# Output product of a hybrid encoder layer: two token passes of 384 and 192 tokens in place of 320 and 256

## The reference, cut to what matters

```python
h = rmsnorm(x, p['norm_pre'])
proj = h @ p['w_in']
...
merged = (ga * (ya.astype(dt) @ p['w_proj_a']) + gb * (yb.astype(dt) @ p['w_proj_b'])
          + gc * (yc.astype(dt) @ p['w_proj_c']))
y = merged.astype(dt) @ p['w_out']
return x + rmsnorm(y, p['norm_post']), (c, n, m, s_h, s_r, shift)
```

## Time and profile before

| | |
|---|---|
| median of three runs | 2294.66 us (2294.58, 2294.66, 6939.04) |
| the profiled execution | 2294.08 us |
| its span, first to last instruction | 2292.3 us |
| mean granted clock of TensorE | 0.999 |
| TensorE matmuls busy | 2251.2 us, 98% |
| VectorE, ScalarE busy | 1271.9 us, 764.1 us |

### The profile page before, as it was taken

How to read it: one execution, slowest core, us unless ns; L and a number is a source line. 1 busy time by engine, 2 the same in 40 slices (tenths; PEclk the granted TensorE clock), 3 DMA queues, 4 the chain that set the end, 5 groups by cost and what they waited for, 6 DMA issues and landing times.

```text
span 2292.3 us, 45143 instructions
## 1 busy us (share of the span) xinstructions
PE 2251.2 (98%) x19061; PEld 2187.7 (95%) x19061; DVE 1271.9 (55%) x1978; ACT 764.1 (33%) x1159; POOL 56.5 (2%) x83
## 2 busy tenths in 40 slices
PE   5999999999999999999999999999999999999998
PEld 5999999999999999998998999989999999999998
DVE  5434443487777776663643735536557664455354
ACT  5321221234333433332422313324323343334443
POOL 0000000000000000000000000000000000000000
PEclk9999999999999999999999999999999999999999
DMA  5422222233342433411311112114221254444365
GB/s 174 140 70 94 88 76 87 73 103 119 112 142 95 137 119 124 156 60 50 106 43 65 72 49 93 61 49 149 75 86 58 90 181 147 156 144 166 141 214 189
DMA packets 65915, 249.40 MB, mean 109 GB/s; under 512 B 8922, under 2 KB 16268, under 8 KB 47892
## 3 DMA queue, kind: packets, MB, share of 16 engines
q1 hardware_dynamic: 65764, 247.14, 31.2%
HBM read 216.92 MB, written 30.19 MB: 108 GB/s over the span
## 4 chain that ended last, share of the span: by engine, by line
PE 95%; DVE 2%; DMA 1%; ACT 1%; issue 1%; SPq 0%; DVEq 0%; POOL 0%; ACTq 0%; POOLq 0%
PE acc L976 56%; PE acc L1135 12%; PE branch L1135 6%; PE acc L1526 6%; PE branch L1526 2%; PE branch L1248 1%; PE branch L1239 1%; PE branch L1223 1%; PE branch L1436 1%; DMA scratch<-in_x_all 1%; PE branch L1080 1%; DVE act_lo L2811 0%; PE branch L1073 0%; PE branch L1212 0%; PE branch L1541 0%
## 5 line engine op out<-in xcount | busy, mean ns | idle before, releaser
L976 PE MATMUL acc<-act_hi,w_hi 128*128 128x320 f32 (+3 forms) x3200 | 975.5, 305 | 1.9 <-DVE act_lo L2811 1.8
L976 PE MATMUL acc<-act_lo,w_hi 128*128 128x320 f32 (+3 forms) x3200 | 948.6, 296 | 0.0
L976 PE MATMUL acc<-act_hi,w_lo 128*128 128x320 f32 (+3 forms) x3200 | 948.1, 296 | 0.0
L976 PEld LDWEIGHTS acc<-act_hi,w_hi 128*128 128x128 f32 x3200 | 602.7, 188 | 16.8 <-issue 5.0
L976 PEld LDWEIGHTS acc<-act_lo,w_hi 128*128 128x128 f32 x3200 | 602.9, 188 | 0.7
L976 PEld LDWEIGHTS acc<-act_hi,w_lo 128*128 128x128 f32 x3200 | 602.7, 188 | 0.0
L2041 DVE TENSOR_TENSOR w_lo<-w_raw,w_hi 128x2048 fp32r<-128x2048 f32 x131 | 300.0, 2290 | 281.1 <-ACT w_hi L1573 278.6
L1573 ACT ACTIVATE w_hi<-w_raw 128x2048 fp32r<-128x2048 f32 x131 | 250.9, 1915 | 134.3 <-PE branch L1526 120.8
L1135 PE MATMUL acc<-corner_terms,w_hi 128*128 128x288 f32 x624 | 125.5, 295 | 0.0
L1135 PE MATMUL acc<-act_hi,w_hi 128*128 128x288 f32 x392 | 115.9, 296 | 1.3 <-DVE w_lo L2231 1.3
L1135 PE MATMUL acc<-act_lo,w_hi 128*128 128x288 f32 x392 | 115.7, 295 | 0.0
(11 more groups left out here) (446 smaller groups left out, 3256.5 us busy)
## 6 DMA issues: line engine op xcount, KB each, us to landing
w_raw<-in_w_stream SPq DMA_DIRECT2D x132, 1024.0 KB, 5.0
w_raw<-in_w_stream SPq DMA_DIRECT2D x76, 512.0 KB, 5.7
gate_logits<-gate_out SPq DMA_DIRECT2D x48, 288.0 KB, 2.3
scratch<-gate_logits SPq DMA_DIRECT2D x48, 288.0 KB, 5.3
scratch<-in_x_all SPq DMA_DIRECT2D x9, 512.0 KB, 6.3
branch_rows<-branch_out SPq DMA_DIRECT2D x16, 288.0 KB, 2.2
scratch<-in_x_all SPq DMA_DIRECT2D x3, 1024.0 KB, 10.5
out_y_prompt<-scratch SPq DMA_DIRECT2D x6, 512.0 KB, 2.9
```

What stands on the lines that cost most here:

```text
L976: last = mm(acc[s][:, at:at + hi - lo], a[:, s, w], b[:, k, lo:hi], start=(k == order[0] and a is whi and b is xh), stop=(k == order[-1] a ...
```

## The change

The first pass takes 384 tokens and the second 192. The 384 tokens are three full groups of 128; the 192 are one of 128 and one of 64. Everything that followed from the old cut follows the new one.

```diff
-OUT_COLS = [(0, 320), (320, KEPT)]
-OUT_ROWS = [[(0, 128), (128, 256), (256, 320)], [(320, 448), (448, KEPT)]]
+OUT_COLS = [(0, 384), (384, KEPT)]
+OUT_ROWS = [[(0, 128), (128, 256), (256, 384)], [(384, 512), (512, KEPT)]]
...
-        zt = [gbuf[0][:, 0:320], gbuf[1][:, 0:320]]
+        zt = [gbuf[0][:, 0:384], gbuf[1][:, 0:384]]
...
-                if p == 0:
-                    last = v.tensor_tensor(YT[0:64, 2, bass.ds(col, P)], br[j][0:64, 2 * P:3 * P], part[0:64], ALU.mult)
+                if p:
+                    last = v.tensor_tensor(YT[0:64, 4, bass.ds(col, P)], br[j][0:64, P:2 * P], part[0:64], ALU.mult)
...
-            v.tensor_reduce(out=small[:, 24:26], in_=squares[:, 0:2, :], axis=AX.X, op=ALU.add).then_inc(out_sums[0], 1)
-            v.tensor_reduce(out=small[0:64, 26:27], in_=squares[0:64, 2:3, :], axis=AX.X, op=ALU.add).then_inc(out_sums[0], 1)
+            v.tensor_reduce(out=small[:, 24:27], in_=squares[:, 0:3, :], axis=AX.X, op=ALU.add).then_inc(out_sums[0], 1)
...
-            v.tensor_reduce(out=small[:, 27:29], in_=squares[:, 3:5, :], axis=AX.X, op=ALU.add).then_inc(out_sums[1], 1)
+            v.tensor_reduce(out=small[:, 27:28], in_=squares[:, 3:4, :], axis=AX.X, op=ALU.add).then_inc(out_sums[1], 1)
+            v.tensor_reduce(out=small[0:64, 28:29], in_=squares[0:64, 4:5, :], axis=AX.X, op=ALU.add).then_inc(out_sums[1], 1)
...
-            pool.wait_ge(out_sums[0], 2)
+            pool.wait_ge(out_sums[0], 1)
             row_scales(0, (0, 3))
-            pool.wait_ge(out_sums[1], 1)
+            pool.wait_ge(out_sums[1], 2)
             row_scales(1, (3, 5))
```

## The result

The changed kernel takes 2315.2 us (median of 4 runs, 2312.6 to 2317.9), the kernel before 2295.3 beside it (median of 4 runs, one of which took 6939.0 us and the others 2294.6 to 2296.0): ratio 1.0084, 95% interval 1.0072 to 1.0096. So it is slower by 19.9 us, inside the 2% that were called "no change" beforehand, but clear of zero. Forecast were 2309.0 us and a range of 2301 to 2316. The profiled execution of the change took 2317.93 us, the longest of the four.

A forecast was written before the change was run, and what follows sets the result against it. TensorE's matmul stream was taken to bound the kernel. Pass one +20.3, pass two -6.2, supply +1.0 and end -0.3 sum to +14.8 us on the profiled 2294.08 us: 2309.0 us, range 2301 to 2316.

The forecast's parts named there:

- The bound: Whole run: TensorE has a matmul in flight for 2251.2 of 2292.3 us, so its stream sets the run time.
- The load floor: Pass two at 192 columns: one 128 x 128 weight load, about 110 ns, sets the matmul spacing, not the stream's 90.0.
- Pass one, +20.3 us: Output product at 384 columns: 723 matmuls on the chain each cost 28.1 ns more, +20.3 us.
- Pass two, -6.2 us: Output product at 192 columns: 768 matmuls go from 118.1 to 110 ns, -6.2 us; products of 5.50 us hide conversion.
- The supply, +1.0 us: Pass two's weight loads: TensorE waits where a landing takes over 7.4 us; +1.0 us, bounds 0 and +4.
- The end, -0.3 us: After the last product: shorter last copy, transposes and squares, last stores of 256 KB; -0.3 us, between 0 and -0.8.
- The case given 0.75: Whole run: load floor of 106 to 113 ns with little or no supply wait, 2305 to 2313 us; chance 0.75.
- the one given 0.10: Whole run: load floor near 118 ns, or a supply wait of over 3 us, 2313 to 2317 us; chance 0.10.
- Conversion decides: Pass two: no load floor, weight-tile conversion holds products at 4.8 us; 2297.8 us, or some 2302 with short supply; chance 0.09.
- no change: Both passes: matmuls cost columns plus a constant, so the paces' sum stays as now; 2292.5 us; chance 0.04.
- Load as dear as the present pace: Pass two: load floor near 118 ns, so no gain there; 2314.1 us; shares the 0.10 with long supply waits.
- The clock rival: Pass two: TensorE drops to 1.2 GHz, 171 ns a matmul, +40.6 us, about 2355 us in all; chance 0.02.

The follow-up runs named there:

- first experiment: Changed kernel with pass one's matmuls cut back to 320 columns, tokens 320 to 383 left out, pass two kept at 192: 2294.2 us, ratio 0.9994.
- the weights-only run: Changed kernel without pass two's residual loads (groups 3 to 5) and stores (groups 1 to 3), TensorE's pass-two loop written out: 2312.6 us.
- the run without stores: Changed kernel without pass two's stores of the three finished row groups, residual loads kept: 2311.7 us, ratio 1.0066.
- the wait at its use: Changed kernel with TensorE's pass-two loop written out and the wait for emptied transpose banks moved to before the transposes: 2313.7 us, ratio 1.0074.

## Why the prediction was right, point by point

**The bound.** Right: TensorE's stream is the chain, and what it gained the run gained.

**The load floor.** Right, and it is what sets the sign. The trace of before showed it at two restarts (0.11 us); the runs at 224, 192 and 128 columns show one pace, 111 to 112 ns (at 240 line and floor can't be told apart). I took 110; a product of 5.56 us against 5.50 forecast makes 16 x 0.06 = 1.0 us. The 106.7 ns of the Trainium skill ("TensorE: Matmul & The Clock Gate", section "LDWEIGHTS (loading the stationary operand)") lie some 5 ns under the measured pace. The formula of the Trainium skill, same title, section "Back-to-back issue gap", by which the sum wouldn't change, doesn't hold here: 224 columns have the pace of 128. The prediction took it alone; the same section gives it for an isolated matmul and says that in a stream of weight loads and matmuls both set the spacing, and with that the runs agree.

**Pass one, +20.3 us.** Right in mechanism, a little small: 8.777 us a product against 8.70 forecast, so +21.5 us. The line through 256, 288 and 320 columns gave 174.3 ns at 384, and 176 was measured. Why the last 64 columns cost 29.8 ns and the ones before 28.1 stays open. It isn't the third transpose, now of 128 rows: with it and 320 columns a product takes 7.35 us (first experiment). And it begins at once: 336 and 352 columns measure 154.4 and 161.0 ns, where the line has 153.2 and 160.3.

**Pass two, -6.2 us.** Half wrong. With nothing in its way it is -5.3 us (89.07 against 94.33, the weights-only run). But the step "the product of 5.50 us hides what must fit in it" failed at the loop's end: the wait `rows_taken` ends with VectorE's `rows_out`, 0.4 us behind the conversion that I did count, and the branch behind it needs more than what is left. That costs 1.7 us in the traces (90.81 - 89.07, the run without stores against the weights-only run).

**The supply, +1.0 us.** The term that was off most. In the profiled execution it is 4.2 us (95.00 - 90.81): one load after 9.6 us, where over 7.4 was named as the point from which TensorE waits. The wait behind it is longer by the branch as well. Two more things were missed: that it is the stores that delay a load, and that this wait of 2.5 us is followed by a stretch at 1.2 GHz, which costs some 1.7 us more (3.4 us at half speed). In the medians it is 3.5 us (2315.2 - 2311.7).

**The end, -0.3 us.** Nothing: the last store landed after 2.9 us at 256 KB as at 512 KB, and the time from the last copy to the end is 11.2 us in both.

The profiled sum: +21.5 (pass one), -5.3 (pass two at its floor), +1.7 (loop), +4.2 (supply and clock), and 1.7 up to the first copy of pass one, nearly all of it ahead of the change; together 23.8 us, the difference of the two spans. Against the forecast's +14.8 the misses are 1.2 (pass one), 0.9 (floor), 1.7 (loop), 3.2 (supply), 0.3 (end) and 1.7 (start): all of one sign.

**The range.** It held with 0.8 us to spare, and the profiled execution lies above it. The case given 0.75, 2305 to 2313 us with little supply wait, didn't come; the measured time is in the one given 0.10 (2313 to 2317), for one of its two reasons, a supply wait of over 3 us. Direction, mechanism and the price of pass one were read rightly. That the other terms' misses stopped short of 2316 was luck.

**The rivals.** "Conversion decides" and "no change" fell with the floor. "Load as dear as the present pace" (2314.1 us) came nearest the time but for a wrong reason: the floor is 112, not 118, and waits eat the difference. The clock rival didn't decide at 192 columns, but was no fancy: in four traces the clock fell to half behind waits of 1.6 to 2.5 us, and at 128 columns that cost up to some 45 us. But no such wait is certain to do it: in the trace of 336 and 240 columns TensorE waited 2.2 us (up to 2257.57 us) and the granted clock stayed at 1.00, and a wait of 1.81 us kept it in one trace and lost it in another (first experiment). What decides between the two stays open. And the rival was priced too low: it doubled the columns and forgot that the load's floor doubles too. At 0.50 matmuls of 192 columns started 213 ns apart, not 171, so a whole pass at the lower level would have cost 768 x (213 - 118.1) = +72.9 us, not +40.6.

## What to carry to other kernels

When each matmul reloads its weights, look for the load's own spacing where the stream restarts; a split of columns that puts any pass below that spacing pays in full for the columns that it moves and gets back only what lies above the spacing (here 5.3 us at best for 21.5). A shorter period also meets waits that were hidden by tenths: list all that must fit in it, with the loop's branch, and the slowest landing, not the median one. And price a wait of TensorE with the clock that can fall behind it.

## What the runs showed of the hardware that was not expected

- A weight load of 1 MB lands in 4.6 to 5.0 us alone (the weights-only run), 4.8 to 6.1 beside 512 KB reads (the run without stores), and up to 9.6 just ahead of stores to memory (the change).
- Behind waits of 1.6 to 2.5 us the granted clock went to 0.50 in four traces (the change, pass one at 320, pass two at 128, the wait at its use), and behind one of 2.2 us (the 336 run) and one of 1.8 us (the kernel before) it didn't. With 192 columns a matmul it was back at 1.00 within the same product, after 3 to 7 us; with 128 columns it stayed at 0.50 for the nine products that were left, in the run that was profiled.
- A 128 x 128 load costs 0.11 us at the full clock and 0.21 at the half, with 128 columns and with 192: the load's floor scales with TensorE's clock.
- A loop's branch behind a semaphore wait brings TensorE's next matmul 0.70 us after the wait ends; the same wait without the branch, 0.05 us.
- A last store of 112 rows landed after 4.0 us, the last stores of 128 and of 64 rows after 2.9.
